# Seven quarter products for product 3 in the convolution groups, interleaved with product 4's

## The reference

```
h = rmsnorm(x, norm_g)
b, c, xv, z, q, k, v, z_b, g_a, g_b = split(h @ w_in)
y_a = (silu(z) * b * conv3(c * xv)) @ w_a_out
y_b = (norm(retention(rope(q), rope(k), v)) * silu(z_b)) @ w_b_out
out = rmsnorm(x + (sigmoid(g_a) * y_a + sigmoid(g_b) * y_b) @ w_o, final_g)
```

## Time and profile before

| | us |
|---|---|
| median of 3 runs | 1368.03 |
| lowest, highest | 1367.47, 1368.32 |
| span of the profiled execution | 1366.5 |
| what lies around the span, against the median | 1.5 |

### The profile page before, as it was taken

The page is one execution under the profiler, slowest core; times in us unless marked ns, Lnnn a source line. Parts: engine busy times, 40 slices in busy tenths (PEclk is TensorE's granted clock), DMA queues, the critical chain, the costliest instruction groups (busy, mean ns, idle before and its releaser), DMA issues.

```text
span 1366.5 us, 16902 instructions
## 1 busy us (share of the span) xinstructions
PE 1354.6 (99%) x6498; PEld 1138.4 (83%) x6498; DVE 1063.1 (78%) x1053; ACT 591.4 (43%) x801; POOL 473.3 (35%) x349
## 2 busy tenths in 40 slices
PE   9999999999999999999999999999999999999997
PEld 7888888888888888888888888888888888888886
DVE  6898474578877777788888888747776998788887
ACT  7843233323222233234333333438778434433445
POOL 0100232244555554555555666415454001100002
PEclk9999999999999999999999999999999999999999
DMA  9746313322212222355443444657767699945443
GB/s 338 215 128 216 114 56 124 124 77 77 77 50 63 74 62 62 109 154 154 138 140 124 116 146 141 198 193 254 264 229 261 142 327 312 233 164 200 161 86 124
DMA packets 106128, 212.74 MB, mean 156 GB/s; under 512 B 6977, under 2 KB 49089, under 8 KB 101185
## 3 DMA queue, kind: packets, MB, share of 16 engines
q1 hardware_dynamic: 103024, 193.82, 42.4%
q0 software_dynamic: 2880, 17.83, 6.6%
q10 hardware_dynamic: 144, 0.02, 0.0%
HBM read 148.20 MB, written 55.05 MB: 149 GB/s over the span
## 4 chain that ended last, share of the span: by engine, by line
PE 95%; issue 1%; ACT 1%; DVE 1%; POOL 1%; DMA 0%; SPq 0%; POOLq 0%; DVEq 0%; ACTq 0%
PE psum L2488 16%; PE psum L2489 16%; PE psum L2486 16%; PE psum L2623 7%; PE psum L2625 7%; PE psum L2624 7%; PE psum L2413 4%; PE psum L2415 4%; PE psum L2416 4%; PE psum L2430 2%; PE psum L2432 2%; PE psum L2431 2%; PE psum L2531 2%; PE psum L2533 2%; PE psum L2532 2%
## 5 line engine op out<-in xcount | busy, mean ns | idle before, releaser
L2488 PE MATMUL psum<-hc,slots 128*128 128x512 f32 x976 | 379.8, 389 | 0.0
L2486 PE MATMUL psum<-hc,slots 128*128 128x512 f32 x976 | 379.8, 389 | 0.0
L2489 PE MATMUL psum<-hc,slots 128*128 128x512 f32 x976 | 379.8, 389 | 0.0
L1088 ACT ACTIVATE slots<-work 128x1024 fp32r<-128x1024 f32 (+1 forms) x158 | 162.0, 1036 | 435.9 <-PE psum L2489 329.0
L1583 DVE TENSOR_TENSOR slots<-work,slots 128x1024 fp32r<-128x1024 f32 (+1 forms) x158 | 228.6, 1448 | 39.0 <-ACT slots L1088 39.0
L2489 PEld LDWEIGHTS psum<-hc,slots 128*128 128x128 f32 x976 | 183.2, 188 | 38.1
L2486 PEld LDWEIGHTS psum<-hc,slots 128*128 128x128 f32 x976 | 183.2, 188 | 37.5
L2488 PEld LDWEIGHTS psum<-hc,slots 128*128 128x128 f32 x976 | 183.2, 188 | 37.3
L1348 ACT ACTIVATE last_slot<-arena 128x1024 fp32r<-128x1024 f32 x112 | 118.6, 1062 | 163.0 <-PE psum L2625 156.8
L2623 PE MATMUL psum<-last_slot 128*128 128x512 f32 (+1 forms) x452 | 175.3, 388 | 0.0
L2625 PE MATMUL psum<-last_slot 128*128 128x512 f32 (+1 forms) x452 | 175.0, 387 | 0.0
(11 more groups left out here) (214 smaller groups left out, 2331.2 us busy)
## 6 DMA issues: line engine op xcount, KB each, us to landing
work<-w_channel SPq DMA_DIRECT2D x80, 512.0 KB, 3.7
arena<-w_last SPq DMA_DIRECT2D x19, 1024.0 KB, 7.5
qk<-qk_scratch SPq DMA_DIRECT2D x32, 512.0 KB, 3.4
arena<-w_last POOLq DMA_DIRECT2D x9, 1024.0 KB, 11.4
v_raw<-value_scratch SPq DMA_DIRECT2D x32, 256.0 KB, 3.7
arena<-gate_scratch SPq DMA_DIRECT2D x16, 512.0 KB, 7.1
value_c<-w_value SPq DMA_DIRECT2D x10, 512.0 KB, 4.8
rows_of_x<-x_rows SPq DMA_DIRECT2D x8, 512.0 KB, 8.8
```

Source lines behind the costliest of these rows:

```text
L1088: nc.scalar.activation(slots[:, u % SLOTS, 0, 0:columns_of(u)], src, ACT.Copy).then_inc(w_hi, 1)
L2486: nc.tensor.matmul(bank, slot[:, 0, w], x_high, start=product in STARTS and j == 0, stop=False, skip_group_check=True)
L2488: nc.tensor.matmul(bank, slot[:, 0, w], x_low, start=False, stop=False, skip_group_check=True)
L2489: last = nc.tensor.matmul(bank, slot[:, 1, w], x_high, start=False, stop=j == 3, skip_group_check=True)
```

## The change

In the eight convolution groups product 3 is divided into seven quarter products too. Its two halves alternate with product 4's: where the order of units was 3, 4 first half, 4 second half, it is now 3 first half (called 3a below), 4 first half (4a), 3 second half (3b), 4 second half (4b). Its x combinations are made once from the kept x quadrant, in group 1, and stay on chip in areas that convolution groups leave free; the T3 combination overwrites a quarter that is put back by DMA for group 10. DVE gets another second_first and second_rest, POOL another second_sums, ACT and DVE one more weight split. The late conv_product moves from ahead of second_first to behind low(6'), the late sigmoid on ACT (late_gate) and the store of y on SP move as well. The products' partial sums use PSUM banks of the next group's products 1 and 6, which therefore wait for the adds.

The four on product 3's weights (work0) are new and stand ahead of product 4's; s1 (L920, L878 before) still follows them. The core of the diff (helpers that only count semaphores are left out):

```
 TWICE = range(1, GROUPS - 1)
-UNIT_TABLE = [(g, p) for g in range(GROUPS) for p in range(8 if g in TWICE else 7)]
+THIRDS = CONVS
+LAST_HALF, THIRD_HALF = 7, 8
+UNIT_TABLE = [(g, p) for g in range(GROUPS) for p in (0, 1, 2, 3, 4, 5, 6, THIRD_HALF, LAST_HALF)
+              if (p != THIRD_HALF or g in THIRDS) and (p != LAST_HALF or g in TWICE)]
...
+def halved_product(g, product):
+    return product == 4 and g in TWICE or product == 3 and g in THIRDS
+def product_at(n):
+    return 3 if n == THIRD_HALF else ORDER[min(n, 6)]
 def columns_of(u):
-    return 3 * QUARTER if u >= VALUE_UNITS and place_of(u)[0] in TWICE and place_of(u)[1] == 6 else 2 * HALF
+    if u < VALUE_UNITS:
+        return 2 * HALF
+    g, n = place_of(u)
+    return 3 * QUARTER if n in (5, 6) and halved_product(g, product_at(n)) else 2 * HALF
...
+    t3_quarters = sb("t3_quarters", CONS_AT, [P, 4, 2, QUARTER])
+    t3_sums = sb("t3_sums", CONS_AT + 10 * KB, [P, 4, 2, QUARTER])
+    third_parts = {name: sb(f"third_{name}", at, [P, 2, 2, QUARTER], F32R)
+                   for name, at in (("T2", TP_AT[0] + 12 * KB), ("T4", TP_AT[1] + 12 * KB), ("T1", CONS_AT + 14 * KB))}
...
             if g == TWICE.stop:
                 sp.wait_ge(unit_done, ended_at(g - 1) + 1)
                 for part in range(2):
-                    sp.dma_start(t4_part(1, part).bitcast(F32), kept_d[:, part]).then_inc(x_in[4], 16)
+                    sp.dma_start(x_quarter(4, 1, part).bitcast(F32), kept_d[0, :, part]).then_inc(kept_in, 16)
+            if g == THIRDS.stop:
+                sp.wait_ge(unit_done, third_ended_at(g - 1) + 1)
+                for part in range(2):
+                    sp.dma_start(x_quarter(3, 1, part).bitcast(F32), kept_d[1, :, part]).then_inc(third_kept, 16)
             if g + 1 < GROUPS:
                 sp.wait_ge(w_ready, unit_at(g, 5) + 1)
                 load_work(g + 1, "d", 3)
                 sp.wait_ge(w_ready, unit_at(g, 7) + 1)
                 load_work(g + 1, "b", 2)
-                sp.wait_ge(w_ready, unit_at(g, 3) + 1)
+                if g in THIRDS and g > THIRDS.start:
+                    stores[kind_of(g - 1)](g - 1)
+                sp.wait_ge(w_ready, third_ended_at(g) + 1)
                 load_work(g + 1, "c", 1)
-            if g:
+            if g and g not in THIRDS:
                 stores[kind_of(g - 1)](g - 1)
             if g == QZS.start:
...
                 conv_gate(g - 1, 2)
             if turned:
                 silu(g - 1, 3)
+            if g in THIRDS:
+                second_sums(g, 3)
             if g in TWICE:
-                second_sums(g)
+                second_sums(g, 4)
             if turn:
                 silu(g, 0)
...
-                product = ORDER[min(n, 6)]
+                product = product_at(n)
                 role = {1: "a", 6: "a", 2: "c", 5: "e", 7: "b", 3: "a", 4: "d"}[product]
-                if n == 7:
-                    act.wait_ge(summed, second_summed(g, 4))
+                if n in (LAST_HALF, THIRD_HALF):
+                    act.wait_ge(summed, second_summed(g, product, 4))
                 elif product in (1, 2, 4):
                     act.wait_ge(work_in[ROLES[g][role]], 16 * LOADED[g + 1][ROLES[g][role]])
                 else:
...
+        def third_high(name):
+            act.wait_ge(t_made, 20 + 8)
+            if name == "T3":
+                act.wait_ge(unit_done, unit_at(THIRDS.start - 1, 3) + 1)
+                act.wait_ge(third_kept, 48)
+            elif name == "T1":
+                act.wait_ge(h_ready, made(3) + 4 + 2)
+            else:
+                m = int(name == "T4")
+                act.wait_ge(tp_out[m], 16 * tp_stored(m))
+            nc.scalar.activation(second_part(3, name, 0), t3_sums[:, ("T1", "T3", "T2", "T4").index(name)], ACT.Copy)\
                 .then_inc(h_hi, 1)
...
+        def late_gate(g):
+            after(g, 3)
+            nc.scalar.activation(gate_z[:, HALF:T], tp_first[g % 2][:, 1, :], ACT.Sigmoid).then_inc(z_sig, 1)
...
         for u in range(12, UNITS + 5):
+            if VALUE_UNITS <= u < UNITS and place_of(u)[1] == LAST_HALF and place_of(u)[0] in THIRDS:
+                late_gate(place_of(u)[0])
             if u + 2 < UNITS:
                 high(u + 2)
...
                     second_high(name)
             if g == TWICE.start and p == 2:
                 second_high("T3")
+            if g == THIRDS.start and p == 2:
+                third_high("T2")
+                third_high("T4")
+                third_high("T3")
+            if g == THIRDS.start and p == 4:
+                third_high("T1")
             if 0 < g <= GROUPS:
                 kind = kind_of(g - 1)
...
                     gate(g, tp_v2, 7)
                 if p == 6:
                     gate(g, tp_first, 3)
-            if kind == "conv" and p == 6:
-                after(g, 3)
-                nc.scalar.activation(gate_z[:, HALF:T], tp_first[g % 2][:, 1, :], ACT.Sigmoid).then_inc(z_sig, 1)
             if g == GROUPS - 1:
...
+        def second_first(g, product):
+            dve.wait_ge(unit_done, unit_at(g, product) + 1)
+            at = (tp_v if product == 4 else tp_first)[g % 2][:, 0, 0:QUARTER]
+            nc.vector.tensor_tensor(at, psum[:, second_bank(g, product), 0:QUARTER], at, ALU.add).then_inc(value_sum, 1)
+        def second_rest(g, product):
+            dve.wait_ge(unit_done, (ended_at(g) if product == 4 else third_ended_at(g)) + 1)
+            z = second_bank(g, product)
+            to = flat((tp_v if product == 4 else tp_first)[g % 2][:, :, :]).rearrange("p (n c) -> p n c", n=4)
             for n, (quarters, bank, c) in enumerate(((slice(1, 4), z, 0), (slice(1, 4, 2), z + 1, 0),
                                                      (slice(2, 4), z + 1, QUARTER))):
                 if n:
-                    dve.wait_ge(value_sum, second_added(g, 1 + n))
-                at = v[:, quarters, :]
-                product = psum[:, bank:bank + 1, c:c + QUARTER].broadcast_to([P, 2 if n else 3, QUARTER])
-                nc.vector.tensor_tensor(at, product, at, ALU.add).then_inc(value_sum, 1)
+                    dve.wait_ge(value_sum, second_added(g, product, 1 + n))
...
                 g, n = place_of(u - 1)
-                if n == 6 and g in TWICE:
-                    second_first(g)
-                elif n == 7:
-                    second_rest(g)
+                if n in (5, 6) and halved_product(g, product_at(n)):
+                    second_first(g, product_at(n))
+                elif n == LAST_HALF:
+                    second_rest(g, 4)
                     low(u + 1)
+                    if g in THIRDS:
+                        conv_product(g, 1)
                     add(g, 4)
+                elif n == THIRD_HALF:
+                    second_rest(g, 3)
+                    add(g, 3)
                 elif ORDER[n] not in (1, 2):
                     add(g, ORDER[n])
-            if u + 2 < UNITS and (u < VALUE_UNITS or place_of(u)[1] < 7):
+            if u + 2 < UNITS and (u < VALUE_UNITS or place_of(u)[1] != LAST_HALF):
...
+            if g == THIRDS.start - 1 and p in (1, 2):
+                for n in range(2):
+                    t3_quarter(2 * (p - 1) + n)
+            if g == THIRDS.start - 1 and p in (4, 5):
+                for name in (("T1", "T3"), ("T2", "T4"))[p - 4]:
+                    t_sum(name, t3_quarters, t3_sums, 20)
+            if g == THIRDS.start and p == 3:
+                for name in ("T2", "T4", "T3"):
+                    third_low(name)
+            if g == THIRDS.start and p == 4:
+                third_low("T1")
...
             if kind_of(g) == "conv":
                 if p == 3:
                     conv_early(g)
-                if p == 6:
-                    conv_product(g, 1)
             if g == GROUPS - 1:
                 if p in (4, 5):
                     retention_begins(p - 4)
...
+        def first_half(g, product):
+            u, z = unit_at(g, product), second_bank(g, product)
             pe.wait_ge(w_ready, u + 1)
-            pe.wait_ge(sum_made, 5 * g + sums_until(ORDER, 7))
-            if g == TWICE.start:
+            pe.wait_ge(sum_made, 5 * g + sums_until(ORDER, before(ORDER, product)))
+            if product == 4 and g == TWICE.start:
                 pe.wait_ge(h_ready, made(3) + 4)
-            product_of_quarters(u, 0, quarter(0), one_six, start=True)
-            product_of_quarters(u, 1, quarter(2), c11)
-            product_of_quarters(u, 2, second("T4"), c21).then_inc(unit_done, 1)
-            pe.wait_ge(w_ready, u + 2)
-            product_of_quarters(u + 1, 2, second("T1"), five, start=True)
-            product_of_quarters(u + 1, 3, second("T3"), seven, start=True)
-            product_of_quarters(u + 1, 1, quarter(3), c12)
-            pe.wait_ge(value_sum, second_added(g, 1))
-            product_of_quarters(u + 1, 0, second("T2"), one_six).then_inc(unit_done, 1)
+            if product == 3:
```

(32 more changed lines are left out.)

## The result

The changed kernel takes 1377.15 us (median of 5 runs, 1376.87 to 1377.32); beside it the kernel before took 1368.28 (1367.47 to 1368.49). The ratio is 1.0063, 95% interval 1.0053 to 1.0074: 0.6% slower. Its profiled execution spans 1375.2 us, 8.8 more than before's 1366.5 (8.78 ahead of rounding). Of each kernel one execution was profiled, and what stands ahead of group 1, above all the value stage, which no edit touches, does not take the same time in all: the first matmul of group 1 starts at 200.05 before and at 199.59 here, and between 199.11 and 200.73 in the thirteen profiled executions.

The account below looks back on a forecast made before the run. PE was taken as the bound. Eight groups at 1.25 wait less 0.49 gain, plus 7 x 0.05, made 6.4 us longer: span 1372.9, with 1.5 around it 1374.4 us; range 1366.5 to 1378.

Parts of the forecast that it names:

- The mechanism: At the group border, DVE and POOL block each other; the low part of product 6 starts 1.63 us later.
- the timetable: Ready times at the border to the next group, in us from the end of product 7, built from profile rows.
- both chains to low(6'): DVE's adds (14.05) and POOL's s1, s3, s2 with ACT's high part (about 14.0) precede next product 6's low part.
- The break-even rival: Next product 1's low part gets through ahead of s1; PE's wait is 0.39, total 1367.2 us; chance 0.14.
- The term for the wait: PE waits 1.25 us at the next group's product 5 for the add of product 6, eight times.
- the lateness of 6': PE waits 0.1 to 0.2 us at the next group's product 6, swallowed by the wait at product 5.
- The 0.05 at product 7': The next group's product 7 waits another 0.05 us for conv_early, in seven groups.
- The gain: On PE, product 3 as quarter matmuls takes 4.95 instead of 5.44 us: 0.49 less in each of eight groups.
- a bound for this: If all 42 quarter matmuls run at 0.120 us, PE takes 0.1 us more a group.
- The setup: The new x combinations and their DMAs in groups 1 and 2, costed at nothing.
- two earlier releases: If next products 7 and 5 must each be released a weight load earlier, 3 us more.
- The signs named beforehand: Group 4 on PE about 38.4 us, 37.1 busy; eight 1.2 us waits; product 1's low part 2.7 us.

Follow-up runs that it names:

- The narrow gates: The changed kernel with POOL's three gate multiplications of each convolution group cut from 512 to 8 columns: 1366.94 us.
- The cuts: The changed kernel with product 3's three shared adds cut to 8 columns, 1376.80 us; with s1 cut to 8 instead, 1379.93; with both, 1365.94.

## Why the prediction was right, point by point

**The mechanism held at every step of the timetable.** It had low(1') blocked by s1 and ending at 8.25; it ends 312.34 - 304.02 = 8.32. s3 10.50: 10.59. s2 12.86: 12.97. Low(6') from 14.05: 14.21. The block lengths came from the old rows (1.08 behind a POOL operation, 2.25 behind a DVE one) and the same lengths came back at every new meeting (1.07, 2.27). The end of the add of product 6, 17.40 into the group, is 17.51. The narrow gates show that these lengths are POOL's doing, which the prediction had only inferred.

**That both chains to low(6') arrive together** was worked out as 14.0 and 14.05. The cuts show it: one alone brings next to nothing, both 11.2 us. The break-even rival, in which low(1') gets through ahead of s1, was not tried in a run of its own; the rows show only that s1 begins 0.74 us before low(1') is ready (308.86 and 309.60).

**The term for the wait was mis-sized, 1.25 for 1.36.** Predicted was one wait at 5' that swallows the lateness of 6'. Measured: 1.20 at 5' and 0.16 at 6'. The sum of rounded ends was 0.1 short at the add, since each step was a few hundredths longer than I took it. The 0.05 at product 7' is not to be seen: the wait at 5' is longer, and product 7' moves along with it.

**The gain was mis-sized, 0.49 for 0.42.** Product 3's 42 quarter matmuls take 5.01 us and product 4's 4.96, where the sum had 4.95 for either. I had a bound for this (0.1 us a group if all 42 take 0.120) and took its lower end; the upper end would have been nearer for product 3.

**The setup was costed at nothing, and costs 0.96 us** (0.69 in group 1, 0.27 in group 2). I had said that the combinations lie where "there is no convolution work behind them". Of group 1 this is true, but its product 4 is already one of quarters, and its second_first waits in the same DVE queue; of group 2 it is not, since conv_early is convolution work. The step that failed is the one where I should have named what is queued behind the added instruction and who waits for it. Moving them took the waits away.

Together: 7 x 0.22 (the group is 1.03 longer, not 0.81), 0.15 in group 10, 0.69 in group 1 and 0.40 in group 2 (0.27 of it the setup, 0.07 the slower quarters), less the 0.45 by which group 1 started earlier in this execution: 2.3 us, and 6.4 + 2.3 is within 0.1 of the 8.8 by which the spans differ. Around the span of the changed kernel lie 1.8 us (1377.03 against 1375.2) where the forecast took 1.5. The forecast of 1374.4 was 2.8 too low; the result stayed inside the range, whose upper end, 1378, had room for slower quarters and for two earlier releases, not for a setup.

The signs named beforehand were eight waits on the add of product 6 of some 1.2 us (eight, 0.97 by the list, 1.20 by the spacing), 2.7 us for low(1') (2.74), low(6') 4.2 in (4.24), and 38.4 us a group (38.64). One did not come as written: PE was to be busy in 37.1 us of the group, and the view gives 37.67. It counts as busy what a matmul comes late without an idle time on record, 0.16 at 6' and 0.24 at 5', so most of the difference is lateness and not work. The list of PE's waits before also has a third row of a microsecond, for POOL's small at L850 (1.1 us, once), which the reading left out; the changed kernel has the same wait, and it plays no part.

**What the prediction did not ask** is whether the loss belongs to the change or to a place in DVE's order. It had all that was needed: the add of product 6 reads PSUM and is not blocked, its product is ready for it at 20.98 of the timetable, and it stood behind two taps whose result nobody on PE waits for until later. Moving it ahead gives back 7.8 us of 8.9.

## What to carry to other kernels

When an engine that was not the bound (the one whose own work sets the time) gets a second piece of work in a stretch where it already has no idle time, look at the end of its queue there, and put the one operation that the bound engine waits for ahead of those that nobody waits for, before taking work away. Where two chains reach one point at the same time, removing either tells next to nothing; cost both, or cut both. Setup work in a "quiet" group is only free if the small operations behind it in the same queue are.

## What the runs showed of the hardware that I had not expected

- **Less work on one side can make the other's block longer.** A DVE operation with two SBUF inputs that is ready 0.74 us after s1 has begun lasts 2.74 us; with s1 cut to 8 columns it meets s3, begun 0.40 before, and lasts 3.08. In both cases it ends 1.07 to 1.08 us after the other has ended. So what counts is how long the running operation still has (1.67 and 2.00 us), not how much there is in all. The first tap (TENSOR_SCALAR, with one tensor input) is held as well: 1.78 beside a gate, 0.80 without. The Trainium skill, SBUF - State Buffer, section Who interferes with whom, describes the two engines as excluding each other while an instruction runs; for the two-input operations these rows agree with it.
- **A block is passed on.** Taking the first tap off DVE (1.8 us) brought the add of product 6 forward by some 0.8 only, since the second tap took over the meeting with the gate (1.28 to 2.31).
- **A late release costs beyond its wait.** Behind each wait the second matmul comes 0.31 to 0.34 us after the first instead of 0.227, so 0.08 to 0.11 us is lost that the list of waits does not show; with the part ahead of the first matmul, eight waits listed at 0.96 cost 1.20 each.
- **An order can cost clock.** After waits of 3.9 us PE's matmuls of 512 columns were 0.43 us apart six to eight times in a row, behind eight waits of eight; after waits of 2.4 us seven to twelve times, behind four of eight (granted clock 0.56 and 0.53 in the two windows read); after the 1 us waits of the changed kernel never. Why four of the eight and not the others was not tried.
